# Sample value products of paged attention: from pages by column group to heads by column group

## What is computed

```python
def _attend(q, k_sel, v_sel, valid):
    s = jnp.einsum('bthd,btkhd->bthk', q, k_sel).astype(jnp.float32) * (HEAD_DIM_A ** -0.5)
    s = jnp.where(valid[:, :, None, :], s, -1e30)
    p = jax.nn.softmax(s, axis=-1).astype(v_sel.dtype)
    return jnp.einsum('bthk,btkhd->bthd', p, v_sel)
```

## Time and profile before

| what | value |
|---|---|
| median of 3 runs | 2079.43 us |
| the runs | 2072.51 to 2079.6 us |
| the profiled execution, its own time | 2083.24 us |
| its span, first to last instruction | 2081.4 us |
| mean granted TensorE clock | 0.979 |
| TensorE matmul busy | 2015.0 us, 97% |
| VectorE busy | 1067.4 us, 51% |
| ScalarE busy | 731.2 us, 35% |
| the loop over the sample sequences | 803.4 to 918.5 us of the span |

### The profile page before, as it was taken

How to read it: one execution, slowest core, us unless ns; L and a number is a source line. 1 busy time by engine, 2 the same in 40 slices (tenths; PEclk the granted TensorE clock), 3 DMA queues, 4 the chain that set the end, 5 groups by cost and what they waited for, 6 DMA issues and landing times.

```text
span 2081.4 us, 37859 instructions
## 1 busy us (share of the span) xinstructions
PE 2015.0 (97%) x15611; PEld 1815.1 (87%) x15611; DVE 1067.4 (51%) x1271; ACT 731.2 (35%) x962; POOL 49.2 (2%) x65
## 2 busy tenths in 40 slices
PE   7999989999988999999999999999999999999996
PEld 7999766578864666679999999999999999999996
DVE  5655976468772431044445554445544445444444
ACT  4333201432222211044444444444444444333332
POOL 1000002200000000000000000000000000000000
PEclk9999999999996999999999999999999999999998
DMA  5544357334564688954446554444444444545553
GB/s 230 179 159 159 111 186 175 88 116 135 165 238 177 238 325 337 365 191 162 161 166 213 192 183 165 161 163 170 171 162 161 165 172 161 193 161 165 165 166 115
DMA packets 95559, 378.12 MB, mean 182 GB/s; under 512 B 26098, under 2 KB 35954, under 8 KB 68082
## 3 DMA queue, kind: packets, MB, share of 16 engines
q1 hardware_dynamic: 70738, 346.88, 47.6%
q0 software_dynamic: 4736, 18.80, 2.8%
q10 hardware_dynamic: 20000, 11.28, 2.0%
HBM read 359.30 MB, written 17.58 MB: 181 GB/s over the span
## 4 chain that ended last, share of the span: by engine, by line
PE 86%; DVE 4%; DMA 3%; SPq 3%; issue 2%; ACT 1%; DVEq 0%; ACTq 0%
PE ps L1011 13%; PE ps L1012 13%; PE ps L1013 13%; PE ps L448 13%; PE ps L966 5%; PE ps L967 5%; PE ps L968 5%; PE ps L482 2%; PE ps L483 2%; PE ps L484 2%; DMA arena<-in_kT 2%; PE ps L873 2%; PE ps L922 1%; SPq L359 1%; SPq L360 1%
## 5 line engine op out<-in xcount | busy, mean ns | idle before, releaser
L1922 DVE TENSOR_TENSOR weights_lo<-ring,weights_hi 128x2048 fp32r<-128x2048 f32 (+1 forms) x152 | 305.7, 2011 | 284.8 <-ACT weights_hi L1445 284.8
L1012 PE MATMUL ps<-h_lo,weights_hi 128*128 128x288 f32 x1408 | 416.1, 296 | 0.0
L1011 PE MATMUL ps<-h_hi,weights_hi 128*128 128x288 f32 x1408 | 414.6, 294 | 0.4 <-DVE weights_lo L1922 0.4
L1013 PE MATMUL ps<-h_hi,weights_lo 128*128 128x288 f32 x1408 | 412.5, 293 | 0.0
L448 PE MATMUL ps<-hT,ring 128*128 128x288 f32 x1472 | 386.5, 415 | 0.0
L1445 ACT ACTIVATE weights_hi<-ring 128x2048 fp32r<-128x2048 f32 (+1 forms) x152 | 257.1, 1691 | 365.8 <-PE ps L1013 353.1
L448 PEld LDWEIGHTS ps<-hT,ring 128*128 128x128 f32 x1472 | 275.9, 192 | 79.2 <-issue 6.5
L1013 PEld LDWEIGHTS ps<-h_hi,weights_lo 128*128 128x128 f32 x1408 | 265.1, 188 | 0.0
L1011 PEld LDWEIGHTS ps<-h_hi,weights_hi 128*128 128x128 f32 x1408 | 264.2, 188 | 0.7 <-DVE weights_lo L1922 0.7
L1012 PEld LDWEIGHTS ps<-h_lo,weights_hi 128*128 128x128 f32 x1408 | 264.4, 188 | 0.1
L1011 PE MATMUL ps<-act_hi,weights_hi 128*128 128x288 f32 x704 | 208.4, 296 | 0.0
(11 more groups left out here) (346 smaller groups left out, 2974.4 us busy)
## 6 DMA issues: line engine op xcount, KB each, us to landing
ring<-in_wst SPq DMA_DIRECT2D x209, 1024.0 KB, 4.9
ring<-in_wdn SPq DMA_DIRECT2D x64, 704.0 KB, 4.1
arena<-in_kT SPq DMA_DIRECT2D x64, 512.0 KB, 7.2
arena<-in_v SPq DMA_DIRECT2D x64, 512.0 KB, 5.7
arena<-chunk_ar_bk ACTq DMA_DIRECT2D x24, 256.0 KB, 3.9
arena<-in_ki SPq DMA_DIRECT2D x64, 64.0 KB, 1.9
arena<-in_xT SPq DMA_DIRECT2D x4, 592.0 KB, 6.7
hT<-in_xT POOLq DMA_DIRECT2D x1, 2304.0 KB, 14.4
```

The lines of the kernel that those rows point to most:

```text
L1011: mm(out, W_HI[:, (u - U_FF) % 2, w], hi, start=start, stop=False)
L1012: mm(out, W_HI[:, (u - U_FF) % 2, w], lo, start=False, stop=False)
L1013: return mm(out, W_LO[:, u % 4, w], hi, start=False, stop=stop)
L1922: tt(W_LO[:, u % 4, 0:m], raw, W_HI[:, at, 0:m].bitcast(F32), ALU.subtract).then_inc(sem("w_split"), 1)
```

## The change

The four column groups now hold pairs of heads. Group g has heads 2g and 2g+1, and all 8 pages are added up in it, with 256 value columns moving. The result of a sequence fills 256 columns of one bank (`ps[5]` or `ps[6]`, by `b` % 2) in place of 512 columns of two. One copy on ScalarE takes it out; VectorE's copy is gone. `OR` is double-buffered by `b` % 2. Each group now holds all 32 rows of weights for its two heads, so that rows of other heads must be dropped: a new constant `own` (one column) zeroes them in the reciprocal `RCP` before `PICK` is made, with one more VectorE instruction at `b` = 0. `out_turn` becomes two products, for the even and the odd head of each pair, with 16 columns moving. The waits `or_half0` and `or_half1` become `or_out`, and `pv_done` counts one for each sequence.

```diff
-        OR, PICK, NMR = area(25344, HA * DH), area(26368, NB, NSAMP), area(26624, NSAMP)
+        OR, PICK, NMR = area(25344, 2, 2 * P), area(26368, NB, NSAMP), area(26624, NSAMP)
...
-                    sp.wait_ge(sem("pv_done"), 2 * (b + 1))
+                    sp.wait_ge(sem("pv_done"), b + 1)
...
-                for half in range(2):
-                    pe.wait_ge(sem(f"or_half{half}"), b)
-                w, v = PTS[b % 2], VG[b % 2]
-                for c in range(2):
-                    for half in range(2):
-                        for j in range(4):
-                            mm(ps[5 + c][32 * j:32 * j + 32, :], w[:, half, 32 * j:32 * j + 32],
-                               v[:, 2 * j + half, c * 512:(c + 1) * 512], start=(half == 0),
-                               stop=False, skip_group_check=True)
-                    for j in range(4):
-                        ins = mm(ps[5 + c][32 * j:32 * j + 32, j * P:(j + 1) * P], w[0:NSAMP, 2, 0:NSAMP],
-                                 VS[0:NSAMP, c * 512 + j * P:c * 512 + (j + 1) * P], start=False, stop=True,
-                                 tile_position=(0, 32 * j), skip_group_check=True)
-                    ins.then_inc(sem("pv_done"), 1)
+                if b >= 2:
+                    pe.wait_ge(sem("or_out"), b - 1)
+                w, v, bank = PTS[b % 2], VG[b % 2], ps[5 + b % 2]
+                for page in range(NPG):
+                    j, half = page // 2, page % 2
+                    for g in range(4):
+                        mm(bank[32 * g:32 * g + 32, 0:2 * P], w[:, half, 32 * j:32 * j + 32],
+                           v[:, page, 2 * g * P:2 * (g + 1) * P], start=(page == 0), stop=False, skip_group_check=True)
+                for g in range(4):
+                    ins = mm(bank[32 * g:32 * g + 32, 0:2 * P], w[0:NSAMP, 2, 0:NSAMP],
+                             VS[0:NSAMP, 2 * g * P:2 * (g + 1) * P], start=False, stop=True, tile_position=(0, 32 * g),
+                             skip_group_check=True)
+                ins.then_inc(sem("pv_done"), 1)
...
-                for h in range(HA):
-                    if h % 4 == 0:
-                        pe.wait_ge(sem(f"or_half{h // 4}"), b + 1)
-                    ins = mm(ps[7][:, h * NS:(h + 1) * NS], OR[:, h * P:(h + 1) * P],
-                             PICK[:, b, h * NS:(h + 1) * NS], start=True, stop=True)
+                pe.wait_ge(sem("or_out"), b + 1)
+                for e in range(2):
+                    ins = mm(ps[7][:, 0:NSAMP].rearrange("p (g e t) -> p g e t", e=2, t=NS)[:, :, e, :],
+                             OR[:, b % 2, e * P:(e + 1) * P],
+                             PICK[:, b, :].rearrange("p (g e t) -> p g e t", e=2, t=NS)[:, :, e, :],
+                             start=True, stop=True)
...
-                act.wait_ge(sem("pv_done"), 2 * b + 2)
-                fn(OR[:, 512:], ps[6][:, :], ACT.Copy).then_inc(sem("or_half1"), 1)
+                act.wait_ge(sem("pv_done"), b + 1)
+                fn(OR[:, b % 2, :], ps[5 + b % 2][:, 0:2 * P], ACT.Copy).then_inc(sem("or_out"), 1)
...
-            def half_out(b):
-
-                dve.wait_ge(sem("pv_done"), 2 * b + 1)
-                cp(OR[:, 0:512], ps[5][:, :]).then_inc(sem("or_half0"), 1)
...
-                half_out(b)
                 if b == 0:
                     dve.wait_ge(sem("den"), 1)
                     ch(nc.vector.reciprocal(RCP, ps[2][:, P + NB:P + 2 * NB]))
+                    ch(ts(RCP, RCP, c_("own"), None, ALU.mult))
```

More of the change, by code:

```diff
@@ L54 @@
                ("ropeI", 128), ("cosI", NT), ("sinI", NT), ("gmask", 64), ("negtri", 512),
-               ("negblk", 36), ("spread", 128), ("wmask", 128), ("dmask", 32), ("oneseq", NB + 1), ("pick", NSAMP),
+               ("negblk", 36), ("spread", 128), ("wmask", 128), ("dmask", 32), ("oneseq", NB + 1), ("pick", NSAMP), ("own", 1),
                ("keep", NT), ("smask", 64), ("eyeb", 32), ("krow", 1), ("seqm", NB)):
@@ L110, in constants @@
     put("pick", np.tile(np.eye(NSAMP), (4, 1)))
+    put("own", np.concatenate([np.arange(NSAMP) // (2 * NS) == g for g in range(4)])[:, None])
     first = np.concatenate([np.arange(SEQ) % CH, np.arange(NSAMP) % NS])
```

## The result

| | before | after |
|---|---|---|
| runs, first comparison | 6 | 6 |
| median, us | 2081.07 | 2065.31 |
| lowest to highest, us | 2072.51 to 2084.07 | 2059.13 to 2071.65 |
| profiled execution, its own time, us | 2083.24 | 2071.65 |
| its span, us | 2081.4 | 2069.9 |

The ratio of the times is 0.9931, with a 95% interval of 0.9909 to 0.9953: faster by 14.4 us, with 9.8 to 18.9 as the interval. A second comparison, 12 runs against 35, gave a ratio of 0.9935 (0.9915 to 0.9954) with medians of 2068.05 and 2080.71. The forecast was 2068.2 us, a gain of 11.2, which lies inside both intervals.

A forecast was written before the change was run, and what follows sets the result against it. TensorE, busy 97% of the span, was taken to bound the kernel. Seven sequences at 1.27 + 0.23 give 10.5 us, less 0.24, plus 0.92: gain 11.2, from 2079.43 to 2068.2 us, range 2060 to 2077.

The forecast's parts named there:

- The last step: Line 937, each turn: 4 records at 0.107 us take 0.43 us, not less, in place of 1.70; gain 1.27.
- The value products: Value products of each turn: 3.61 + 0.57 = 4.18 us in place of 4.41, a gain of 0.23.
- The rival of unhidden loads: Value products: loads in the additional rounds not hidden, up to 1.04 us more per sequence; 2071 to 2078 us; chance 0.13.
- the estimate from the Trainium skill: Value products: about 60 cycles overhead per matmul, 25 ns for each of 32 additional records, 0.8 us a turn.
- The recorded lower bound of 3.95 us: Value products, if the rounds kept only line 922's time per column: some 3.95 us, a gain of 0.45.
- Copies, banks: Copies on VectorE and ScalarE in sequences 0 to 6: under the 3.99 us half gate tile, costing nothing; no wait.
- Sequence 0: Making of PICK: one more VectorE instruction between the reciprocal and line 1888, charged 0.24 us, uncovered.
- Sequence 7: Last sequence, copy uncovered: 0.58 us wait, then 0.43 and 0.11, 1.12 us; gain 0.69, plus 0.23 from value products.
- Transfers: Value pages in the loop: 5.7 us left in hand; rival of lateness 2073 us, chance 0.08 shared with later deadlines.
- The sum: Whole kernel: seven sequences give 10.5 us, sequence 0 costs 0.24, sequence 7 gives 0.92; gain 11.2 us.
- a clock that no longer falls: Half gate tile of sequence 1: low clock stretch vanishes, 1.7 us more gained, 2066.5 us; chance 0.10.
- the line of 0.5%: Whole time: faster means below 2069.0 us; chances 0.52 faster, 0.44 within 0.5%, 0.04 slower.

The follow-up runs named there:

- The two experiments with the product counts exchanged: Changed kernel with eight last-step products: 2082.4 us, ratio 1.0014; kernel before with two last-step products: 2069.88 us, ratio 0.9949.
- the run group by group: Changed kernel with the value-product loops exchanged, all 8 pages of one column group before the next group: 2131.19 us in one run.
- one bank: Changed kernel with one bank and one buffer OR for all sequences, in place of two in turn: 2067.12 us, ratio 0.9936.
- early `PICK`: Changed kernel with the sums' product and the making of PICK ahead of sequence 0's second half gate tile: 2067.27 us, ratio 0.9955.
- no late pages: Changed kernel without loading the value pages of sequences 2 to 7, those of 0 and 1 used again: 2069.45 us, ratio 0.9948.

## Why the prediction was right

*The last step.* Forecast 0.43 us, measured 0.36. The mechanism, a price by the count of records and not by their columns, held; the size was a little too dear, and "not less" was wrong. Between 4 and 16 records each costs 0.112 us ((1.70 - 0.36) / 12), and the first load begins 0.24 us ahead of the step, under the gate tile's products (867.15 against 867.39), so the mean of 16 did not carry over to 4. The two experiments with the product counts exchanged give 1.34 us a turn both ways. This is 10.7 of the loop's gain.

*The value products.* Forecast 4.18, measured 4.16, from 3.59 and 0.57 against the 3.61 and 0.57 taken from the scores' rows. The rival of unhidden loads and the estimate from the Trainium skill, page TensorEngine Tiling (Array Packing), section Instruction Overhead, both fall: the run group by group shows one record of 256 columns each 0.21 us (12 in 2.57), 16 of which are 3.4 us. Four groups beside each other took 3.59, so that 0.2 us is left for all else, and no extra 0.8. The recorded lower bound of 3.95 us does not follow from its row: 3.71 for line 922 and 0.57 for the new keys are 4.28.

*Copies, banks.* Priced at nothing, and nothing: one bank gives the same turn, and with the last step as before the turn was 14.40, just the 0.25 of the value products below 14.65, which leaves nothing for the copy that is gone.

*Sequence 0.* Forecast 0.24 more, measured 0.26 (a wait of 1.05 against 0.79), and hideable, as the early `PICK` shows.

*Sequence 7.* Forecast 1.12 us from where TensorE's next instruction could have begun to the merge. That is 0.57 behind 905.39, at 905.96, and to 907.06 it is 1.10. Part of the agreement is luck: the copy began 0.14 and took 0.38 as forecast, but the hand-over back took 0.14 and not 0.06 (906.48 to 906.62), and the last step 0.44 and not 0.54. The prediction also read the turn from sequence 6 to 7 wrongly: it has no transposes, but a half gate tile more, and took 18.03 us before and 16.44 after. It cost the sum nothing, since that half is the same in both.

*Transfers.* Two shorter turns were to leave 5.7 us in hand; at least 6.6 were left, at 399 and 409 GB/s over whole turns. The Trainium skill, page DMA: Bandwidth & Descriptors, section Where 436 GB/s comes from, has about 358 GB/s as the HBM limit of a core; this launch on a single core moved more over whole turns, so here the measurement decides against it as a limit.

*The sum.* The instructions of the loop gained 11.9 us: 13.56 between the two profiles, less the 1.7 of the low clock in the first. The forecast was 11.2, the 0.07 us a turn of the last step being most of what it lacked. The forecast also let the first profile's low stretch stand on both sides; it expected a loop of 104 us, and the profiles show 101.5, which is its own rival of a clock that no longer falls (chance 0.10). I took one profile's low stretch for a fixed property of both kernels, when the kernel before shows it in one profile of sequence 0 and not in the next two, one of which has a low stretch behind the loop instead.

Whether the change makes such stretches rarer is not settled. The count over 13 profiles speaks for it and would be worth about 1.6 us on average. The times don't show it. Six comparisons have 4 records in the last step: the changed kernel twice, two products on the old value products, early `PICK`, one bank, and no late pages. By the ratios, the gain lies above what the loop's instructions give by 2.5, 1.7, 0.6, -3.8, 1.5 and -1.0 us, 0.2 in the mean, each with some 4 us either way and some with the same runs of the kernel before. The gains of 14.4 and 13.5 us are thus 11.9 with chance on top, and 11.9 lies inside both intervals.

*The number.* That the second median, 2068.05, meets the forecast's 2068.2 to 0.2 us is luck. The forecast started from a median of three runs, 2079.43, and in the larger comparison the kernel before had 2080.71.

*The chances.* I set the line of 0.5% at 2069.0 and the forecast 0.8 us below it. The measured gain, 0.69% and 0.65%, lies beyond; both intervals reach to just under 0.5%, so it is not far beyond. Of the signs named for the profile after, the value products (4.16 us) and the wait at sequence 7 (0.60) lay inside what was set, the last step (0.36) and the turn (13.06) just below it.

## What to carry to other kernels

When a product moves a handful of columns, count products, not columns: here an fp32 product with 128 stationary columns was two records, and one record took 0.107 us in a row of 16 with 4 moving columns and 0.09 in a row of 4 with 16. Lay the output of the step before out so that one product serves several heads, even if rows of other heads must be masked away. Before pricing a new tile form, look for the same form in another stage of the same trace; here it gave the value products to 0.02 us. And price an added transfer rate by the time in hand between landing and use, not by the share of the engines.

## What was not expected of the hardware

- Here column groups ran beside each other only where products of different groups stood near in program order. Four groups in turn: 3.59 us for 64 records; group by group: 11.43 us, with overlap for a few records at each border.
- The changed kernel's 12 runs spread by 15 us of 2068 (0.7%) with the mean granted clock between 0.975 and 0.984, while the loop under study repeats to 0.02 us in its profiles. Effects of 1 us are read from the trace.
- A wait of 5.7 us cost another 2.0 us behind it, through the low clock: the value products took 5.60 us for 3.59.
- Cutting the transfers from 399 to 82 GB/s left a turn of 13.06 us where it was.
